# A transformer kernel on one core: unread products in TensorE's waits, and the first softmax maximum moved ahead of gates, key blocks and convolutions

## The chip, the core and the metric

The kernel runs on one core of a Trainium2 chip, as one program with one launch. TensorE (PE; its weight loads are shown as PEld), VectorE (DVE) and ScalarE (ACT) each run their own instruction list in order and wait for each other by semaphores; SyncE's queue (SP) issues the transfers, GpSimd (POOL) does nothing but four start-up instructions. The metric is the device time of one execution in microseconds (us). The kernel before takes 2849.9 us, the median of 3 runs (2849.38 to 2851.75).

## What is computed

Two blocks follow one another on a sequence of 256 tokens of width 1024, all in f32. The first has two layers of half-step feed-forward, token mixer, half-step feed-forward; the second adds 16 tokens (272 in all) and has an attention, a mixture of experts (MoE), a gated recurrence (`hgrn2`) and a second MoE. Cut to what the change touches:

```python
for l in range(DEPTH):                       # first block, DEPTH = 2
    h = modulate(rms_norm(x, norm_g[l, 0]), ...)
    x = x + 0.5 * gate * swiglu(h, ffn_w_in[l, 0], ffn_w_out[l, 0])
    h = modulate(rms_norm(x, norm_g[l, 1]), ...)
    x = x + gate * token_mix(h, ...)
    h = modulate(rms_norm(x, norm_g[l, 2]), ...)
    x = x + 0.5 * gate * swiglu(h, ffn_w_in[l, 1], ffn_w_out[l, 1])

def token_mix(h, ...):
    qkv, z, b_raw, a_raw, q_n, kc, vc, ks, vs, kw, vw, g_raw = split_cols(h @ w_in, IN_SIZES)
    y_gdn = gated_deltanet(qkv, z, b_raw, a_raw, ...)   # conv, silu, l2 norm; g from a_raw;
                                                        # chunks: (I + lower)^-1, then a scan
    y_nsa = native_sparse_attention(q_n, kc, vc, ...)   # three masked softmax branches:
                                                        # compressed keys, selected, window
    return concatenate([y_gdn, y_nsa]) @ w_out

# in native_sparse_attention
blk = t[:, cmp_idx] + pe[:, None, :]                    # key blocks of 32 tokens, stride 16
k_cmp = silu(blk @ w1) @ w2
# in gated_deltanet
g = -exp(a_log) * softplus(a_raw + dt_bias)             # the gates
```

The recurrence of the second block scans chunks with decayed scores, `o = o_inter + o_intra`, and carries a state.

## The kernel before

A `Block` gives every engine one long list. All engines walk over the same list of stages: `ada` (modulation), then per layer `ffn`, `mix`, `ffn`, then a norm, `fox` (attention), `moe`, `hg` (the recurrence), `moe`. Nothing reorders work afterwards: the order in which each engine's code is written is the order in which it runs. Weights come as slabs of 1 or 2 MB through a ring of 8 slots, issued by SP in one loop (L544) as slots come free.

**Waits.** `mark(ins, q, name, ...)` lets an instruction raise its engine's step semaphore, and `await_(engine, q, name, ...)` waits for that count. An engine stops at a wait with everything that stands behind it.

**Between stages.** The sums of squares of the norm are products with a matrix of ones (`ss_pair`, L1479 is its matmul); ScalarE makes the root from them (L2114, L2115), loads a table (L2156), VectorE scales (L3091), ScalarE shifts (L2121 or L2124), and, ahead of a feed-forward, VectorE makes the low part of a split f32 (L3184). Only then can TensorE begin: in a feed-forward with three products for each split pair (`up_split`, L1500 to L1502), in a mixer with projections (L825).

**In a mixer.** Projections and other products are "jobs" (`run_jobs`), four PSUM banks in turn, each read by ScalarE (L1684) or VectorE. After jobs 0 to 15 come 24 attention units. Unit n is `scores(n)` (PE L1036), `softmax_max(n)` (DVE: mask L2583, maximum L2587, negated L2597), `exp(n)` (ACT L1806), `turn(n)`, a transpose (PE L1053), a copy of it (ACT L1826), `values(n)` (PE L1068) and `output(n)` (DVE L2607 to L2624). `scores(n+1)` waits for the mask of unit n, since it overwrites the bank. Jobs are handed out between units by the table `MIX_STEPS`: 16, 17, 18, ... one for unit 0, one for unit 1 and so on. Jobs 16 and 17 are projections (8 products of 128x256 each); 18 and 19 are products of the key blocks (L775), for which VectorE writes `kp` in `block_keys` (four additions, L2337, behind a memset, L3237, and behind ScalarE's eight copies of `nsa_blocks`, L1790 and L1791). `gdn_gates` makes g (DVE L2318 to L2326, ACT L1657 to L1661), read from job 20 on. `conv(c)` is one of twelve column convolutions on VectorE (L2284, then L2287 three times); columns 0 and 1 are done ahead of `softmax_max(0)`, the others each after its projection.

**Behind the units** comes `gdn` with its levels: for each of 8 matrices products of 32x32 blocks, 32 products a group: L919 (p), L929 (up), L933 (tp), with ScalarE's copy L1733 between the first two. Level 0 waits for `lo` (DVE L2464). `gdn_values` (L888) and `turn_outputs` (L1088) lie between levels.

**In the recurrence** (`hg_scan`), for each of three token tiles t, levels from -1 up: score products (L1172 and others), one job (L816 or L825) behind each; at a tile's end it waits for `hsum` (ACT L1962) before the output products (L1202, L1205).

**Products for the clock** exist already: `keep_clock` (L1236) issues products that nobody reads, ahead of waits in the MoE's token sort.

An f32 product of `nc.tensor.matmul` shows as two MATMUL records and two LDWEIGHTS records in the trace; a product on split operands (`fp32r`, L1500 to L1502) as one of each.

## Time and profile before

| | |
|---|---|
| median of 3 runs | 2849.9 us |
| the profiled execution | 2847.29 us, of which its span 2845.5 us |
| PE busy | 2638.1 us (93%) |
| DVE busy / ACT busy | 1405.4 us (49%) / 775.1 us (27%) |
| mean granted TensorE clock | 0.969 |
| chain that ended last, by engine | PE 86%, DVE 6%, DMA 3%, ACT 3%, issue 1% |
| transfers | 701.51 MB, mean 247 GB/s |

The chain of work that ended last names, at each step back from the end, what released it. A time on it is on the path; idle time of other engines isn't. The line PEclk of the page shows the TensorE clock granted in 40 slices, in tenths of 2.4 GHz; in the table by stretches PEclk 1.00 is 2.4 GHz throughout and 0.50 is 1.2 GHz throughout, the only two levels that the records have.

### The profile page before, as it was taken

The page shows a single profiled execution, that of the slowest core. Times are in us where ns is not written, and L with a number is a line of the kernel's source. Part 1 is how long each engine was busy: PE and PEld are TensorE (multiplying, and loading weights), DVE is VectorE, ACT ScalarE, POOL GpSimd, SP SyncE. Part 2 cuts the span into 40 slices and gives each one's busy share as a digit, 9 for nine tenths or more (in the row PEclk, how much of TensorE's full clock was granted, in tenths as well). Part 3 has the DMA queues.
Part 4 walks back from the last instruction along what each step waited for, and adds up shares of the span by engine and source line. Part 5 has one row for each costly group of instructions (what it writes and reads, how often), then busy time and mean ns, then how long its engine had stood idle before and what let it go on. Part 6 is the DMA issues. An engine that isn't in the chain of part 4 may idle for free.

```text
span 2845.5 us, 44974 instructions
## 1 busy us (share of the span) xinstructions
PE 2638.1 (93%) x18582; PEld 1884.0 (66%) x18582; DVE 1405.4 (49%) x3071; ACT 775.1 (27%) x1473; POOL 0.2 (0%) x4
## 2 busy tenths in 40 slices
PE   6999988999999988999999999999999999999998
PEld 5998767998998767998777533333356784333333
DVE  7875764786773773663233333333324532333333
ACT  3332354334332352442233211111112321111110
POOL 0000000000000000000000000000000000000000
PEclk8999989999999989999999999999999999999999
DMA  8876211674766310454211599999961236999997
GB/s 351 302 277 267 105 46 60 265 297 193 296 268 237 119 60 33 186 222 168 75 67 38 198 377 427 428 427 427 428 243 60 90 119 269 418 428 427 427 428 307
DMA packets 72307, 701.51 MB, mean 247 GB/s; under 512 B 8736, under 2 KB 11424, under 8 KB 11680
## 3 DMA queue, kind: packets, MB, share of 16 engines
q1 hardware_dynamic: 72096, 698.54, 61.1%
q8 instruction: 152, 2.49, 0.3%
q14 instruction: 59, 0.48, 0.0%
HBM read 697.46 MB, written 1.05 MB: 245 GB/s over the span
## 4 chain that ended last, share of the span: by engine, by line
PE 86%; DVE 6%; DMA 3%; ACT 3%; issue 1%; DVEq 0%; SPq 0%; ACTq 0%
PE ps L1299 15%; PE ps L825 11%; PE ps L1500 9%; PE ps L1502 9%; PE ps L1501 9%; PE ps L1324 7%; PE ps L1340 5%; PE ps L816 4%; DMA ring<-slabs 3%; PE ps L1068 2%; PE ps L1269 1%; PE ps L1479 1%; PE ps L807 1%; PE ps L792 1%; PE ps L1053 1%
## 5 line engine op out<-in xcount | busy, mean ns | idle before, releaser
L1500 PE MATMUL ps<-arena_parts 128*128 128x256 f32 x2112 | 602.3, 285 | 35.0 <-DVE arena_parts L3184 35.0
L1502 PE MATMUL ps<-arena_parts,ring_parts 128*128 128x256 f32 x2112 | 598.8, 284 | 0.0
L1501 PE MATMUL ps<-arena_parts 128*128 128x256 f32 x2112 | 597.1, 283 | 0.0
L1299 PE MATMUL ps<-ring,arena 128*64 128x512 f32 x2048 | 467.1, 598 | 0.2 <-DMA ring<-slabs 0.2
L1500 PEld LDWEIGHTS ps<-arena_parts 128*128 128x128 f32 x2112 | 402.1, 190 | 36.6 <-DVE ring_parts L3099 20.7
L1501 PEld LDWEIGHTS ps<-arena_parts 128*128 128x128 f32 x2112 | 404.7, 192 | 0.2
L1502 PEld LDWEIGHTS ps<-arena_parts,ring_parts 128*128 128x128 f32 x2112 | 401.1, 190 | 0.0
L3099 DVE TENSOR_TENSOR ring_parts<-ring,arena_parts 128x2048 fp32r<-128x2048 f32 x132 | 300.9, 2291 | 112.8 <-ACT arena_parts L1647 112.8
L825 PE MATMUL ps<-h,ring 128*128 128x256 f32 (+1 forms) x1408 | 337.1, 398 | 9.4 <-ACT h L2124 5.9
L1647 ACT CAST arena_parts<-ring 128x2048 fp32r<-128x2048 f32 x132 | 250.0, 1904 | 301.1 <-DMA ring<-slabs 293.6
L2946 DVE TENSOR_TENSOR x<-ps,x 128x272 f32<-128x272 f32 x512 | 190.6, 434 | 263.3 <-PE ps L1340 250.7
L825 PEld LDWEIGHTS ps<-h,ring 128*128 128x128 f32 x1408 | 272.8, 197 | 58.2 <-issue 10.9
L1299 PEld LDWEIGHTS ps<-ring,arena 128*64 128x64 f32 x2048 | 136.5, 136 | 253.9 <-issue 253.0
L1324 PE MATMUL ps<-ring,arena 128*64 128x512 f32 x992 | 225.9, 596 | 25.9 <-ACT arena L2020 16.2
L1340 PE MATMUL ps<-arena 64*128 64x272 f32 x1024 | 167.5, 428 | 31.9 <-DVE x L2946 31.9
L2020 ACT ACTIVATE arena<-ps 128x256 f32<-128x256 f32 x64 | 24.6, 384 | 625.8 <-PE ps L1299 625.8
L1324 PEld LDWEIGHTS ps<-ring,arena 128*64 128x64 f32 x992 | 75.7, 136 | 169.8 <-issue 156.6
L732 DVE CUSTOM_DVE_ANT_0 ring<-ring,arena,vectors 128x1024 f32<-128x1024 f32 x144 | 177.0, 1280 | 10.2 <-DMA ring<-slabs 10.2
L1340 PEld LDWEIGHTS ps<-arena 64*128 64x128 f32 x1024 | 82.5, 185 | 140.7 <-DVE x L2946 84.5
L2924 DVE COPY arena<-ps 128x256 f32<-128x256 f32 x64 | 27.2, 425 | 203.5 <-PE ps L1308 203.5
L816 PE MATMUL ps<-ring,h 128*128 128x256 f32 (+3 forms) x576 | 120.0, 367 | 0.0
L816 PEld LDWEIGHTS ps<-ring,h 128*128 128x128 f32 (+1 forms) x576 | 86.6, 179 | 25.7 <-issue 6.8
(409 smaller groups left out, 2435.5 us busy)
## 6 DMA issues: line engine op xcount, KB each, us to landing
ring<-slabs SPq DMA_DIRECT2D x190, 2048.0 KB, 14.5
ring<-slabs SPq DMA_DIRECT2D x278, 1024.0 KB, 5.3
sq<-aside SPq DMA_DIRECT2D x2, 1024.0 KB, 7.9
arena<-aside SPq DMA_DIRECT2D x2, 1024.0 KB, 10.6
x<-xT SPq DMA_DIRECT2D x1, 1024.0 KB, 5.9
outT<-x SPq DMA_DIRECT2D x1, 1024.0 KB, 4.6
constants<-const SPq DMA_DIRECT2D x1, 875.0 KB, 7.8
vectors<-vec SPq DMA_DIRECT2D x1, 647.5 KB, 7.2
```

Source lines behind the costliest of these rows:

```text
L732: ins = nc.vector.tensor_tensor_reduce(out=wt[:, f], in0=wt[:, f], in1=cond_row, scale=1.0, scalar=col("ada_b", l * NADA + n), op0=ALU.mul ...
L816: mm = nc.tensor.matmul(ps[0:size, b, 0:width], rhs[:, k, at:at + size], wt[:, k, c0:c0 + width], start=(k == 0), stop=(k == KC - 1))
L825: mm = nc.tensor.matmul(bank(b, n), wt[:, k, c0:c0 + P], rhs[:, k, 0:n], start=(k == ks[0]), stop=(k == ks[-1]))
L1299: mm = nc.tensor.matmul(ps[W * hh:W * hh + W, e % 2, :], xe[:, e % 2, 4 * k + c], wt[:, c], start=(k == 0 and c == 0), stop=(k == 1 and c ...
L1324: mm = nc.tensor.matmul(ps[W * dh:W * dh + W, 3, :], hide[:, e % 2, j, W * hh:W * hh + W], wt[:, j, 512 * dh:512 * dh + 512], start=(hh == ...
L1340: mm = nc.tensor.matmul(ps[:, 4 + 2 * (i % 2) + dh, 0:T2], ysb[rows64, e % 2, i * P:(i + 1) * P], ge[rows64, e % 2], start=True, stop=True)
L1500: nc.tensor.matmul(out, w_hi, v_hi, start=start, stop=False, skip_group_check=True)
L1501: nc.tensor.matmul(out, w_hi, v_lo, start=False, stop=False, skip_group_check=True)
L1502: return nc.tensor.matmul(out, w_lo, v_hi, start=False, stop=stop, skip_group_check=True)
L1647: nc.scalar.copy(hi_slab(i), slab_view(i)).then_inc(s["w_hi"], 1)
L2946: nc.vector.tensor_tensor(x[:, d], ps[:, 4 + 2 * (i % 2) + dh, 0:T2], x[:, d], ALU.add)\
L3099: nc.vector.tensor_tensor(low_view(i), wt, hi_slab(i).bitcast(F32), ALU.subtract)\
```

## The change

Three things are changed. First, a new helper `unread(b, n)` issues n f32 products of 128x256 on constants into bank b, whose result nobody reads; it waits for nothing and raises nothing. It is called ahead of the first wait of each feed-forward (16 in the first, 8 in the other three), ahead of a mixer's first projections (5), ahead of `gdn` (4), inside `gdn` at level 1 (1 and 4), and in `hg_scan` (5 and 7 at tile 0, 5 at tiles 1 and 2, there behind a wait for `ho` that stood a few lines lower). That is 40 + 10 + 8 + 10 + 22 = 90 products. Second, in both mixers, VectorE does `softmax_max(0)` first, then the gates, and puts memset and key blocks behind `softmax_max(1)` and the convolutions of columns 0 and 1 behind units 1 and 2. Third, ScalarE does the copies of jobs 14 and 15 and `exp(0)` ahead of the gates and `nsa_blocks`. SP's list is the same.

```diff
@@ gdn (PE)
+                    if lev == 1:
+                        unread(6, 1)
                     await_("act", q, "p", lev)
                     await_("dve", q, "t", lev - 1)
...
                     mark(mm, q, "tp", lev)
+                    if lev == 1:
+                        unread(6, 4)
@@ hg_scan (PE)
                         b = 2 + (lev + 1) % 2
+                        if t == 0 and lev < 1:
+                            unread(6, 5 if lev < 0 else 7)
...
+                    if t:
+                        await_("act", q, "ho", t - 1)
+                        unread(6, 5)
                     await_("act", q, "hsum", t)
...
                     if t:
                         await_("dve", q, "hst", t - 1)
-                        await_("act", q, "ho", t - 1)
@@ new helper (PE)
+            def unread(b, n):
+                for _ in range(n):
+                    nc.tensor.matmul(bank(b, T1), ident, const[:, 0:T1], start=True, stop=True)
@@ the stages (PE)
                 if st[0] == "ffn":
+                    unread(2, 8 if t else 16)
...
                     pe.wait_ge(s["tables_in"], 32)
+                    unread(2, 5)
                     run_jobs(q, st, 0, 14, slab, job, h_at=("h_ready", n_ready - KC))
...
                     await_("dve", q, "o", n_units - 1)
+                    unread(6, 4)
                     gdn(q, st[1], st, slab, job)
@@ mixer (ACT)
                     exp, copy = attention(q, st)
-                    gdn_gates(q, st[1])
                     mix_task(q, st, 14)
                     mix_task(q, st, 15)
+                    exp(0)
+                    gdn_gates(q, st[1])
                     nsa_blocks(q, st[1], job)
-                    exp(0)
@@ mixer (DVE)
+                        softmax_max, output = attention(q, st)
+                        softmax_max(0)
                         gdn_gates(q, l)
-                        mark(nc.vector.memset(kp, 0.0), q, "kp0")
-                        await_("dve", q, "kp0")
-                        block_keys(q, l)
-                        softmax_max, output = attention(q, st)
-                        conv(q, l, 0)
-                        conv(q, l, 1)
                         await_("dve", q, "sg")
-                        softmax_max(0)
                         for n_unit in range(24):
                             if n_unit < 23:
                                 softmax_max(n_unit + 1)
                             if n_unit:
                                 output(n_unit - 1)
+                            if n_unit == 0:
+                                mark(nc.vector.memset(kp, 0.0), q, "kp0")
+                                await_("dve", q, "kp0")
+                                block_keys(q, l)
+                            if n_unit in (1, 2):
+                                conv(q, l, n_unit - 1)
```

VectorE's list in the first mixer before, from the last two instructions of the gates to the first softmax maximum (L3237 the memset, L2337 the key blocks, L2284 and L2287 the convolutions of columns 0 and 1, L2583 the mask, L2587 the maximum):

```order
L2322 SCALAR_TENSOR_TENSOR arena<-arena 128x8
L2326 SCALAR_TENSOR_TENSOR arena<-arena 128x8
L3237 MEMSET arena 128x1024
L2337 TENSOR_TENSOR arena<-arena,vectors 128x32x8
L2337 TENSOR_TENSOR arena<-arena,vectors 128x2x15x8
L2337 TENSOR_TENSOR arena<-arena,vectors 128x32x8
L2337 TENSOR_TENSOR arena<-arena,vectors 128x2x15x8
L2284 TENSOR_SCALAR arena<-arena,vectors 128x256
L2287 SCALAR_TENSOR_TENSOR arena<-arena,vectors 128x256 x3
L2284 TENSOR_SCALAR arena<-arena,vectors 128x256
L2287 SCALAR_TENSOR_TENSOR arena<-arena,vectors 128x256 x3
L2583 TENSOR_TENSOR arena<-ps,constants 128x2x128
```

The same place now, where VectorE's line numbers are 16 higher up to the mixer's body (L3251 is the reciprocal before the gates, L2599 the mask, L2603 the maximum, L2613 the negation, L2334 to L2342 the gates, L3262 the memset):

```order
L3251 RECIPROCAL arena<-arena 128x56
L2599 TENSOR_TENSOR arena<-ps,constants 128x2x128
L2603 TENSOR_REDUCE arena<-arena 128x2
L2613 TENSOR_SCALAR arena<-arena 128x2
L2334 TENSOR_TENSOR arena<-arena,vectors 128x8
L2336 SCALAR_TENSOR_TENSOR arena<-arena 128x8
L2338 SCALAR_TENSOR_TENSOR arena<-arena 128x8
L2342 SCALAR_TENSOR_TENSOR arena<-arena 128x8
L2599 TENSOR_TENSOR arena<-ps,constants 128x2x128
L2603 TENSOR_REDUCE arena<-arena 128x2
L2613 TENSOR_SCALAR arena<-arena 128x2
L3262 MEMSET arena 128x1024
```

The mask of unit 0 has moved from behind memset, key blocks and two convolutions to the front of the gates, and the mask of unit 1 stands ahead of the memset too. Behind the memset follow the key blocks, then the convolution of column 2 as before.

TensorE's list before, from the last values of the attention to level 2 of `gdn` (L1068 values, L919, L929 and L933 the groups of 32 small products, L888 the products of `gdn_values`):

```order
L1068 MATMUL ps<-arena 128x64 x4
L919 MATMUL ps<-constants,arena 32x32 x32
L888 MATMUL ps<-constants,arena 128x128 x8
L919 MATMUL ps<-arena 32x32 x32
L929 MATMUL ps<-arena 32x32 x32
L933 MATMUL ps<-arena 32x32 x32
L919 MATMUL ps<-arena 32x32 x32
```

The same place now (L1072 the values, L1249 the unread products, L931 and L935 what were L929 and L933):

```order
L1072 MATMUL ps<-arena 128x64 x4
L1249 MATMUL ps<-constants 128x256 x4
L919 MATMUL ps<-constants,arena 32x32 x32
L888 MATMUL ps<-constants,arena 128x128 x8
L919 MATMUL ps<-arena 32x32 x32
L1249 MATMUL ps<-constants 128x256
L931 MATMUL ps<-arena 32x32 x32
L935 MATMUL ps<-arena 32x32 x32
L1249 MATMUL ps<-constants 128x256 x4
L919 MATMUL ps<-arena 32x32 x32
```

Four products stand between the attention and level 0, one ahead of L931 and four ahead of level 2; nothing else has moved there.

## Rows read from the trace of the kernel before

**Rows 1.** The page, the granted clock in 40 slices.

```profile
PEclk8999989999999989999999999999999999999999
```

**Rows 2.** Waits of TensorE, whole span: line, waited for, us in total, times, longest.

```profile
PE ps L1500 <- DVE arena_parts L3184: 35.0, 4, 20.3
...
PE ps L1036 <- DVE arena L2583: 13.7, 4, 6.0
...
PE ps L825 <- ACT h L2124: 5.9, 2, 2.9
PE ps L1202 <- ACT arena L1962: 5.6, 2, 3.2
```

**Rows 3.** Stretches around the first units: length, busy by engine, PEclk, DMA share, GB/s.

```profile
289.50:295.50 6.00, 0.00 (x1) 0.01 (x1) 5.56 (x14) 0.09 (x1) 0.00 (x0) 0.90 0.01 1
295.50:302.94 7.44, 6.67 (x24) 5.17 (x24) 3.30 (x9) 2.34 (x11) 0.00 (x0) 0.62 0.00 0
...
942.12:946.91 4.79, 0.00 (x2) 0.00 (x1) 4.54 (x12) 0.00 (x0) 0.00 (x0) 0.93 0.03 10
946.91:954.54 7.63, 6.86 (x22) 5.30 (x22) 3.30 (x9) 2.34 (x11) 0.00 (x0) 0.60 0.00 0
```

**Rows 4.** Timeline of the first mixer: start, us, engine, line, operation, idle before.

```profile
285.78 3.72 PE L825 MATMUL ps<-h,ring 128*128 128x256 f32 x16
...
289.69 1.84 DVE L2337 TENSOR_TENSOR arena<-arena,vectors 128x256 f32<-128x256 f32 x4 [1.57 <-ACT arena L1791]
...
295.02 0.42 DVE L2583 TENSOR_TENSOR arena<-ps,constants 128x256 f32<-128x256 f32 x1
...
297.07 0.69 PE L1053 MATMUL ps<-constants,arena 128*128 128x128 f32 x2 [0.77 <-ACT arena L1806]
```

**Rows 5.** VectorE's timeline in the next units, first and last mask.

```profile
303.41 0.42 DVE L2583 TENSOR_TENSOR arena<-ps,constants 128x256 f32<-128x256 f32 x1 [4.16 <-PE ps L1036]
...
316.67 0.69 DVE L2583 TENSOR_TENSOR arena<-ps,constants 128x512 f32<-128x512 f32 x1 [0.87 <-PE ps L1036]
```

**Rows 6.** Stretches behind the waits at stage starts, columns as in rows 3.

```profile
234.86:241.00 6.14, 6.14 (x21) 5.12 (x22) 6.14 (x12) 3.03 (x8) 0.00 (x0) 0.72 0.00 0
...
489.31:493.50 4.19, 4.19 (x24) 4.19 (x25) 4.19 (x8) 4.19 (x5) 0.00 (x0) 0.65 0.00 0
...
690.03:695.00 4.97, 4.97 (x28) 4.97 (x29) 4.97 (x9) 4.97 (x5) 0.00 (x0) 0.64 0.00 0
...
1147.07:1152.00 4.93, 4.93 (x26) 4.93 (x27) 4.93 (x9) 4.93 (x5) 0.00 (x0) 0.60 0.00 0
```

**Rows 7.** TensorE's timeline, products of `keep_clock` at 2.4 GHz.

```profile
1586.90 2.46 PE L1236 MATMUL ps<-h,constants 128*128 128x272 f32 x10
```

**Rows 8.** Around the levels of `gdn`: stretches, then one row of TensorE's timeline.

```profile
406.04:408.25 2.21, 0.00 (x0) 0.03 (x1) 2.01 (x8) 2.19 (x2) 0.00 (x0) 0.50 0.01 4
408.25:425.54 17.29, 13.37 (x656) 11.85 (x657) 10.93 (x21) 3.31 (x10) 0.00 (x0) 0.54 0.02 5
...
1061.60:1079.31 17.71, 12.18 (x657) 10.52 (x657) 10.93 (x21) 3.31 (x10) 0.00 (x0) 0.79 0.01 4
...
416.83 0.44 PE L919 MATMUL ps<-arena 32*32 32x32 f32 x16 [1.53 <-issue]
```

**Rows 9.** The recurrence: two stretches, then rows of the timeline.

```profile
2170.68:2176.39 5.71, 5.71 (x39) 2.55 (x40) 1.62 (x9) 0.89 (x5) 0.00 (x0) 0.70 0.00 0
...
2231.63:2238.88 7.25, 7.25 (x55) 7.13 (x59) 0.00 (x0) 2.76 (x5) 0.00 (x0) 0.76 0.00 0
...
2161.24 7.20 DVE L2737 TENSOR_TENSOR_SCAN arena<-constants,arena 128x16 f32<-128x16 f32 x24
...
2170.68 0.56 PE L1172 MATMUL ps<-arena 128*16 128x16 f32 x16 [3.78 <-DVE arena L2789]
...
2287.78 1.36 DVE L2835 TENSOR_TENSOR h<-arena 128x1152 f32<-128x1152 f32 x1 [12.74 <-ACT arena L1974]
...
2289.63 2.62 PE L792 MATMUL ps<-h,ring 128*128 128x144 f32 x20
```

## The prediction, made before the changed kernel ran

> **What bounds the kernel now.** I read the page's shares first: TensorE is busy 93% and holds 86% of the chain that ended last, so what can be won is its idle time and the time in which it runs at the lower of its two clocks. The 40 slices of the clock [rows 1] show the second: 9 and 8 are spread over nearly the whole span, which reads as many short stretches at 1.2 GHz, one at a time, not as one slow stage.
>
> Next I read TensorE's waits [rows 2]. Four waits of the feed-forwards for L3184 hold 35.0 us, one of them 20.3, so the other three are 4.9 each. Two waits at the mixers' starts for ScalarE's L2124 are 2.9 each. The scores wait for VectorE's mask L2583 up to 6.0 us. Two waits in the recurrence for the row sums L1962 hold 5.6, the longer 3.2.
>
> Last I cut the span into stretches. In the wait of the second scores the clock is still 0.90 and 0.93, and in the 7.4 and 7.6 us behind it 0.62 and 0.60 [rows 3]: the clock falls after TensorE has idled, and the work behind pays. The same stands behind the waits at stage starts: 0.72, 0.65, 0.64, 0.60 [rows 6], and in the recurrence 0.70 and 0.76 [rows 9]. Work behind a wait loses (1 - clock) x length against full clock. Products with nothing to wait for, put into the wait, cost nothing as long as they end before the awaited result comes, and may keep the clock up.
>
> **What an unread product costs.** Ten records of `keep_clock`, five products of 272 columns, take 2.46 us at 2.4 GHz [rows 7], 0.49 each at most; 256 columns make it about 0.44, and at 1.2 GHz 0.87. Five take 2.2 us, seven 3.1, eight 3.5, sixteen 7.0.
>
> **A. VectorE's and ScalarE's order in the mixers.** Between the end of job 16 (289.50) and the start of scores(2) (302.94) lie 6.00 + 7.44 = 13.44 us [rows 3]. Only scores(1), turn(0) and job 17 stand in it. At full clock these are 6.67 x 0.62 = 4.1 us, or from above 3.72 for the job [rows 4], 0.69 / 2 = 0.35 for the turn and as much for the scores: 4.4. I take 4.4. The mask of unit 0 began at 295.02 behind key blocks (289.69) and two convolutions [rows 4]; by the new order it comes right behind the reciprocals, when scores(0) are done, before job 16 ends. `exp(0)`, which stood behind `nsa_blocks`, then also runs beside job 16, so the turn's 0.77 goes too. The gain is 13.4 - 4.4 = 9.0 here and 4.79 + 7.63 - 4.4 = 8.0 in the second mixer: 17.0. (The waits alone, 6.00 + 4.79 + 2 x 0.77, are 12.3; the other 4.7 is the clock.) The new unit 0 must wait for nothing else; about half a microsecond for the turn of unit 0 is my allowance: 16.5.
>
> What is moved back has to be done somewhere. The key blocks (1.84) and the two convolutions (from 289.69 + 1.84 to 295.02) end 5.3 us after they begin [rows 4]; the memset writes as many numbers as the key blocks and is bounded by their 1.84: up to 7.2 us. VectorE idles ahead of the masks of the next four units, first 4.16, last 0.87 us [rows 5], 8.9 in the four. So it fits, narrowly. The key blocks' reader is job 18, in unit 2: VectorE reaches them behind the mask of unit 1, some 6 us earlier in TensorE's work than job 18. The convolutions 0 and 1 and the gates are read only from job 20 on and later. If the cover were gone, masks would be late by what does not fit.
>
> **B. Mixer starts.** Five products, 2.2 us, in a wait of 2.9 [rows 2]: hidden, with 0.7 idle left. The 6.14 us behind ran at 0.72 [rows 6], a loss of 1.7; the second mixer's start is the same work behind the same wait, and I count it alike. Gain 2 x 1.7 = 3.4.
>
> **C. Feed-forward starts.** Eight products, 3.5 us, in waits of 4.9: hidden. Losses behind [rows 6]: 4.19 x 0.35 = 1.5, 4.97 x 0.36 = 1.8, 4.93 x 0.40 = 2.0; sum 5.2. But there TensorE reads what VectorE's L3184 still writes, one of eight parts after another, so a faster clock meets a wait for the next part; I take 4.0. The first feed-forward's sixteen products, 7.0 us in 20.3, leave 13 us idle behind them: 0.
>
> **D. Recurrence.** Tile 0, level -1: VectorE's scan L2737 (7.20 us for 24 [rows 9]) decides when level 0 starts; 0. Level 0: seven products, 3.1 us, in a wait of 3.78, and 5.71 us at 0.70 behind it: 1.7. Tile 1: five, 2.2 us, in a wait of 2.4 (5.6 - 3.2), and 7.25 us at 0.76 behind it: 1.7, less what spills over: 1.6. Tile 2: five in 3.2; L2835 ends at 2287.78 + 1.36 = 2289.14, and TensorE goes on at 2289.63 [rows 9], so faster products there win at most 0.5: 0.5. Sum 3.8.
>
> **E. `gdn`.** Here I expect a loss. Before level 0, TensorE waits 2.21 us with the clock at 0.50 already [rows 8]. The four products start when VectorE's last output is there, so at 0.87 each they take 3.5 us and outlast the wait by at least 1.3; that output ends inside the 2.21 us, which can make it some 0.6 more. I take 1.9 for each of two mixers: +3.8. The level chain behind it is as long at clock 0.54 (17.29 us) as at 0.79 (17.71) [rows 8]: 656 small records, the busy time 13.37 and 12.18, and the rest waits. So TensorE's rate does not set it; one wait reads "issue", 1.53 us [rows 8], that is, the next instructions weren't there. The five products of level 1 (2.2 to 4.3 us) lie beside that idle time, and a better clock gives nothing in the chain. From below, what follows the chain could run faster by what the clock is worth behind it; I estimate up to 1.4 for both. Net +2.4, with ends at +14 (2 x (1.9 + five products at 0.87 and one us for the wait behind them), nothing hidden) and -6 (8 less of the chain, as the third rival has it, beside the 2 that are lost ahead).
>
> The Trainium skill (page "Runtime: NRT & Kernel Launch", section "Instruction fetch mechanics") says that a long program is streamed in 16 KiB pieces and that crossing a boundary is "mostly hidden". The trace does not agree in this chain, with 1.53 us of "issue" in one place. By the page alone the chain would be TensorE's own, and a higher clock would shorten it; that is the third rival below.
>
> **Sum.** B, C and D are 3.4 + 4.0 + 3.8 = 11.2. The clock fell in places with far shorter idle too, so some of these stretches will be slow anyway: I take nine tenths, 10. In all 16.5 + 10 - 2.4 = 24.1. Against the profiled execution, 2847.3, that is 2823.2; the median of the runs is 2.6 higher, 2849.9, and the forecast against it 2825.8, so 2826.
>
> **Rivals.**
> First, the unread products don't hold the clock: they come right after an idle stretch or too few of them count. For it: the trace has no such products in a wait of this kind; those of `keep_clock` run at 2.4 GHz, but in another stage. Against: in the mixer the clock fell only where TensorE idled. Then heads (waits 12.3 and part of the clock, since shorter idle alone may not drop it: 16.5) and `gdn` with its loss: 2849.9 - 16.5 + 2.4 = 2835.8, say 2835.
>
> Second, VectorE's backlog. The moved 7.2 us don't fit into the gaps of 8.9, because with 9 us gone VectorE has lost that idle time too, and masks run late through the first units: up to 7.2 us come back in each mixer. 2826 + 14 = 2840. Against: between units stand more than four gaps.
>
> Third, the chain of `gdn` is TensorE's after all. At full clock its busy 13.37 x 0.54 is 7.2 us, with five products and the short waits some 13 us instead of 17.5: about 4 less for each, 8 for both, less what I took for it: 2819. Against: equal length at 0.54 and 0.79.
>
> Fourth, slower. The products run at 1.2 GHz because the clock has already fallen when they begin, don't raise it, and become the work that is waited for. Price 0.87 each, excess over the waits: feed-forwards 3 x (7.0 - 4.9) = 6, mixers 2 x (4.4 - 2.9) = 3, recurrence 6.1 - 3.8 and 2 x 4.4 - 5.6 and what lies beside L2737, 7 at most; `gdn` 2 x 5.7 = 11: 27. Against A's 16.5 this is +10, 2860. It decides once more than 17 of the 27 lie on the path. For it: the 0.50 in `gdn`. Against: elsewhere the clock was 0.90 and 0.93 in the wait itself [rows 3].
>
> That the change does not do what it says (the wait for the mask is replaced by one for ScalarE's copies of 14 and 15): 2845 to 2850.
>
> **How the numbers follow.** Forecast 0.57, first rival 0.18, second 0.07, third 0.12, fourth 0.03, last 0.03. The forecast's own range is 2820 to 2832, from `gdn`'s ends and B to D at half or whole. The range 2818 to 2838 takes in the first and third rival and leaves out somewhat under 0.2. What a measurement tells from no change is about 0.2%, 5.7 us: faster than 2844.2 has 0.92, the same 0.04, slower 0.04.
>
> **What would show it.** In the changed profile the first mask of each mixer follows the reciprocals at once, and TensorE's scores wait no 6.0 and 4.8 us for it; the stretch from the end of job 16 to scores(2) is 4 to 5 us. The stretches of [rows 6] and those of [rows 9] stand near 1.00, and the waits in [rows 2] read shorter by the products' time (4.9 to 1.4, 2.9 to 0.7). Level 0 of `gdn` begins 1 to 2 us after L2464's result, and its chain stays near 17 us. VectorE's gaps ahead of the masks of units 2 to 5 are nearly gone, but TensorE doesn't wait for them. Wrong would be: clocks of 0.6 to 0.7 behind the products (first rival), waits for masks of units 2 to 6 (second), a chain of 13 us (third), or L1249's records at half clock with the awaited result long there (fourth).

## The result and the profile after

| | before | changed |
|---|---|---|
| median | 2849.6 us | 2825.3 us (4 runs, 2820.5 to 2827.1) |
| ratio | | 0.991 (95%: 0.9893 to 0.9928) |
| profiled execution's span | 2845.5 us | 2823.3 us |
| PE busy | 2638.1 us | 2659.1 us |
| mean granted TensorE clock | 0.969 | 0.979 |

The kernel became 24.3 us faster; the forecast was 2825.8. Five later runs of the same changed kernel gave a median of 2827.1 (ratio 0.9912). TensorE is busy 21 us longer in a span that is 22.2 shorter: it now does 90 products more.

The page's clock slices [rows 1] after:

```profile
PEclk8999989999999999999999999999999999999999
```

Slice 15, which was 8, is 9 now, and nothing else shows: changes over stretches of a few microseconds hardly move a slice of 71. TensorE's waits after [rows 2], of the whole span (us in total, times, longest):

```profile
PE ps L1513 <- DVE arena_parts L3200: 18.3, 4, 14.0
...
PE ps L1040 <- DVE arena L2599: 2.9, 2, 1.4
...
PE ps L825 <- ACT h L2140: 1.5, 2, 0.8
...
PE ps L1210 <- ACT arena L1978: 1.3, 2, 1.1
PE ps L1249 <- DVE hid L2640: 1.2, 2, 0.6
```

The three shorter waits of the feed-forwards went from 4.9 to (18.3 - 14.0) / 3 = 1.4 us, those of the mixers from 2.9 to 0.8. The 6.0 and 4.8 us of the scores for the mask are gone; the 2.9 left on that line are two short waits that stood there before. One wait is new: the products ahead of `gdn` themselves wait 0.6 us for L2640. The stretches that answer to [rows 6], then to [rows 8], then to the two of [rows 9] (length, busy by engine, PEclk, DMA share, GB/s):

```profile
234.80:241.00 6.20, 6.13 (x29) 5.43 (x30) 6.20 (x12) 3.09 (x8) 0.00 (x0) 1.00 0.00 0
485.20:489.40 4.20, 3.64 (x29) 3.67 (x30) 4.20 (x10) 4.20 (x6) 0.00 (x0) 1.00 0.00 0
684.90:689.90 5.00, 4.51 (x36) 4.55 (x37) 5.00 (x9) 5.00 (x6) 0.00 (x0) 1.00 0.01 3
1130.70:1135.60 4.90, 4.79 (x38) 4.82 (x39) 4.90 (x9) 4.90 (x5) 0.00 (x0) 1.00 0.00 0
401.40:419.20 17.80, 12.62 (x667) 10.65 (x667) 9.04 (x17) 3.19 (x9) 0.00 (x0) 0.88 0.02 4
1046.64:1063.98 17.34, 12.41 (x667) 10.45 (x667) 9.04 (x17) 3.19 (x9) 0.00 (x0) 0.89 0.01 4
2150.00:2156.40 6.40, 5.95 (x49) 2.87 (x50) 2.04 (x11) 1.71 (x9) 0.00 (x0) 0.73 0.01 3
2211.30:2218.60 7.30, 7.10 (x117) 6.84 (x117) 1.41 (x6) 3.48 (x6) 0.00 (x0) 1.00 0.01 2
```

Behind every stage's start the clock is 1.00 where it was 0.60 to 0.72, and so it is in the recurrence's tile 1. In tile 0 it is 0.73 where it was 0.70: there the prediction failed, as term D below tells. The level chain of `gdn` has 0.88 and 0.89 for 0.54 and 0.79 and is as long as before.

TensorE in the first mixer, against [rows 4] (start, us, then what the row is):

```profile
285.42 3.72 PE L825 MATMUL ps<-h,ring 128*128 128x256 f32 x16
289.07 0.49 PE L1040 MATMUL ps<-arena 64*128 64x128 f32 x4
289.49 0.44 PE L1057 MATMUL ps<-constants,arena 128*128 128x128 f32 x2
289.76 3.62 PE L825 MATMUL ps<-h,ring 128*128 128x256 f32 x16
293.31 0.49 PE L1040 MATMUL ps<-arena 64*128 64x128 f32 x4
```

No row has an idle time before it, which would stand at its end in brackets. From the end of job 16 (289.1) to scores(2) (293.31) it is 4.2 us, where it was 13.4. VectorE beside it, against [rows 4] and [rows 5]:

```profile
285.53 0.43 DVE L2599 TENSOR_TENSOR arena<-ps,constants 128x256 f32<-128x256 f32 x1 [1.26 <-PE ps L1040]
...
289.67 0.42 DVE L2599 TENSOR_TENSOR arena<-ps,constants 128x256 f32<-128x256 f32 x1 [1.31 <-PE ps L1040]
...
291.86 1.90 DVE L2353 TENSOR_TENSOR arena<-arena,vectors 128x256 f32<-128x256 f32 x4
...
295.40 0.42 DVE L2599 TENSOR_TENSOR arena<-ps,constants 128x256 f32<-128x256 f32 x1
...
304.80 0.68 DVE L2599 TENSOR_TENSOR arena<-ps,constants 128x512 f32<-128x512 f32 x1
```

The masks wait for scores only in units 0 and 1; from 290.9 to 309.8 VectorE works without a gap. The 8.9 us of [rows 5] are used up, and TensorE does not wait for it.

**Where the time went, stretch by stretch.** Each figure is the difference in time between the same two of TensorE's instructions, against the first profile of before. "Again" are second profiles of the same code; the last column is the changed kernel without any product in `gdn`.

| stretch | before again | changed | changed again | order only | products only | no `gdn` products |
|---|---|---|---|---|---|---|
| first mixer's start (50 us) | 0.0 | -0.4 | -1.7 | +1.2 | -1.7 | -0.4 |
| first head (17.5 us) | -0.4 | -9.2 | -9.2 | -9.2 | +1.0 | -9.2 |
| attention behind it, up to its last values | 0.0 | +0.6 | +2.3 | +0.6 | 0.0 | +0.6 |
| ahead of first `gdn` | 0.0 | +2.1 | +2.1 | 0.0 | +2.1 | 0.0 |
| first `gdn`'s chain | +1.1 | +0.5 | +1.6 | +0.4 | +0.6 | +2.3 |
| behind it, to feed-forward | +1.8 | +2.8 | +1.1 | +1.2 | +1.1 | +3.5 |
| three feed-forward starts | -0.1 | -4.1 | -4.1 | -0.3 | -4.1 | -4.1 |
| second mixer's start | 0.0 | -1.7 | -1.7 | 0.0 | -1.7 | -1.7 |
| second head | 0.0 | -8.3 | -8.2 | -8.2 | +0.7 | -8.2 |
| attention, ahead of second `gdn` | 0.0 | +1.0 | +1.1 | -1.1 | +1.8 | -1.1 |
| second `gdn`'s chain | +1.7 | -0.4 | +1.3 | +0.7 | -0.4 | +0.4 |
| behind it | -1.4 | -0.9 | -2.7 | -1.0 | -3.3 | +0.4 |
| `fox` | -0.2 | -3.1 | +0.4 | +3.0 | -1.6 | -3.0 |
| recurrence's three tiles | +1.2 | -1.8 | -1.8 | +1.2 | -1.7 | -3.5 |

The heads with the new order, the feed-forward starts with all their products and the step ahead of the first `gdn` repeat to 0.1 us in every kernel that has the same code there. Most other rows move by 1 to 3.5 us without any change of code.

### The profile page after: what moved, and what is told of

Read it like the earlier page. It is cut to its first block, busy times and chain, and to the rows that moved or that the text cites. A ratio compares the mean times of both kernels' runs of the same rounds, so it can differ in the third digit from the quotient of the medians.

```text
span 2823.3 us, 45331 instructions
## 1 busy us (share of the span) xinstructions
PE 2659.1 (94%) x18762; PEld 1901.8 (67%) x18762; DVE 1404.0 (50%) x3071; ACT 774.9 (27%) x1473; POOL 0.2 (0%) x4
## 4 chain that ended last, share of the span: by engine, by line
PE 85%; DVE 6%; DMA 4%; ACT 3%; issue 1%; DVEq 0%; SPq 0%; ACTq 0%
PE ps L1312 14%; PE ps L825 11%; PE ps L1513 9%; PE ps L1515 9%; PE ps L1514 9%; PE ps L1337 7%; PE ps L1353 5%; DMA ring<-slabs 4%; PE ps L816 4%; PE ps L1072 2%; PE ps L1492 1%; PE ps L1282 1%; PE ps L807 1%; PE ps L792 1%; PE ps L1057 1%
## 5 line engine op out<-in xcount | busy, mean ns | idle before, releaser
L1513 PE MATMUL ps<-arena_parts 128*128 128x256 f32 x2112 | 600.3, 284 | 18.3 <-DVE arena_parts L3200 18.3
L825 PE MATMUL ps<-h,ring 128*128 128x256 f32 (+1 forms) x1408 | 327.0, 390 | 5.0 <-DVE h L3107 3.5
L825 PEld LDWEIGHTS ps<-h,ring 128*128 128x128 f32 x1408 | 265.4, 191 | 50.8 <-issue 6.6
L816 PEld LDWEIGHTS ps<-ring,h 128*128 128x128 f32 (+1 forms) x576 | 85.6, 177 | 24.3 <-issue 4.6
```

Source lines behind the costliest of these rows:

```text
L816: mm = nc.tensor.matmul(ps[0:size, b, 0:width], rhs[:, k, at:at + size], wt[:, k, c0:c0 + width], start=(k == 0), stop=(k == KC - 1))
L825: mm = nc.tensor.matmul(bank(b, n), wt[:, k, c0:c0 + P], rhs[:, k, 0:n], start=(k == ks[0]), stop=(k == ks[-1]))
L1513: nc.tensor.matmul(out, w_hi, v_hi, start=start, stop=False, skip_group_check=True)
```

## The experiments

The diffs are against the changed kernel; `...` stands for lines left out.

**The order alone.** All `unread` calls taken out, the order of the change kept.

```diff
-                    unread(2, 8 if t else 16)
...
-                    unread(2, 5)
...
-                    unread(6, 4)
```

> The new order of VectorE and ScalarE in the mixers, no unread products. Theory (terms add): the order alone gives the 16.5 to 17.8 us that its stretches show, so 2832 to 2833 us against 2849.6. Rival (VectorE's backlog comes back as waits later in the mixer): 2840 or more. Rival (products and order depend on each other, since the clock in the mixers falls again without products): gain under 14 us, 2836 or more.

Measured: 2835.4 us, ratio 0.9946 (0.9932 to 0.9961), 15.4 us won against 2850.8 for before in the same comparison: somewhat less than the 16.5 to 17.8 expected, and more than the rival's 14. Its heads gave 9.2 and 8.2, so the order alone carries the whole of term A. Its waits at the starts stayed:

```profile
PE ps L1506 <- DVE arena_parts L3190: 34.3, 4, 19.7
...
PE ps L825 <- ACT h L2130: 5.8, 2, 2.9
```

No backlog followed. Of 17.4 in the heads 15.4 arrived in the median; the differences that do not repeat (+3.0 in `fox`, for one) cover that.

**The products alone.** The old order of VectorE's and ScalarE's mixer, all 90 products.

```diff
                     exp, copy = attention(q, st)
+                    gdn_gates(q, st[1])
                     mix_task(q, st, 14)
                     mix_task(q, st, 15)
+                    nsa_blocks(q, st[1], job)
                     exp(0)
-                    gdn_gates(q, st[1])
-                    nsa_blocks(q, st[1], job)
...
+                        gdn_gates(q, l)
+                        mark(nc.vector.memset(kp, 0.0), q, "kp0")
+                        await_("dve", q, "kp0")
+                        block_keys(q, l)
                         softmax_max, output = attention(q, st)
+                        conv(q, l, 0)
+                        conv(q, l, 1)
+                        await_("dve", q, "sg")
                         softmax_max(0)
-                        gdn_gates(q, l)
-                        await_("dve", q, "sg")
...
-                            if n_unit == 0:
-                                mark(nc.vector.memset(kp, 0.0), q, "kp0")
-                                await_("dve", q, "kp0")
-                                block_keys(q, l)
-                            if n_unit in (1, 2):
-                                conv(q, l, n_unit - 1)
```

> All 90 unread products, the old order of VectorE and ScalarE. The prediction's terms: 10 won at the stage starts and in the recurrence, 2.4 lost in gdn: 2842. By the changed kernel's trace (gdn cost about 7 us, not 2.4, in the two mixers together): 4 to 5 us won, 2845. Rival (the products hold no clock): 2849.6 + 2.4 or more, 2852.

Measured: 2843.7 us, ratio 0.9976 (0.9963 to 0.9989), 7.1 us won, between the two values expected (2842 and 2845). The products do hold a clock. The parts add: 15.4 + 7.1 = 22.5, against 24.3 for both. The scores' wait is what it was:

```profile
293.95 0.80 PE L1040 MATMUL ps<-arena 64*128 64x128 f32 x4 [5.99 <-DVE arena L2599]
```

Its second `gdn` shows the chain at almost full clock:

```profile
1063.16:1080.50 17.34, 11.93 (x668) 9.98 (x667) 9.27 (x18) 3.19 (x9) 0.00 (x0) 0.98 0.02 4
```

17.34 us at 0.98, with five products more in it, against 17.29 at 0.54 [rows 8].

**Without the products of `gdn`, and without the four ahead of it alone.** In the second kernel only the last of these three calls is taken out.

```diff
-                    if lev == 1:
-                        unread(6, 1)
...
-                    if lev == 1:
-                        unread(6, 4)
...
-                    unread(6, 4)
                     gdn(q, st[1], st, slab, job)
```

> The changed kernel without the nine products of each gdn (four ahead, one and four at level 1); nothing else differs from it. Prediction's term E: 2.4 us faster than the changed kernel, 2823. Changed kernel's trace: 5 to 7 us faster, 2818 to 2820. Rival (the products of gdn pay by a higher clock behind): 2 to 6 us slower, 2827 to 2831.

> The changed kernel without the four products ahead of gdn alone; the one and four at level 1 stay. If the level chain is bound by the supply of its instructions, the five at level 1 cost nothing and the head is the whole loss: as fast as the kernel without any gdn products, within 1 us, 2819 to 2820. If the chain pays for them too: only 4 us of the gain, about 1.5 to 3 us slower than without any.

Measured: 2822.7 us (0.9902, 0.9887 to 0.9918) without any, 2825.7 (0.9916, 0.9903 to 0.993) without the four. Without any product in `gdn` the kernel is 2.6 and 4.4 us faster than the changed kernel's two medians; term E says 2.4. Without the four alone it is no faster than the changed kernel, and 3.0 slower than without any, with runs that nearly separate (2818.6 to 2823.5 without any, 2823.2 to 2828.9 without the four). By the expectation that is a chain that pays for its five products. The traces, of executions only 0.5 us apart (2822.7 and 2823.2), say something else. The first row is the changed kernel's, the second that without the four:

```profile
397.69 3.78 PE L1249 MATMUL ps<-constants 128*128 128x256 f32 x8 [0.62 <-DVE hid L2640]
```

```profile
400.08 1.08 PE L919 MATMUL ps<-constants,arena 32*32 32x32 f32 x64 [2.22 <-DVE arena L2479]
```

The products wait 0.6 and run 3.8 us, at 1.2 GHz, in place of a wait of 2.2: 2.1 us lost in each mixer. The chain without any product is not shorter in the traces: over the seven kernels and repeats without products in `gdn` (14 chains, the changed kernel's variants below included) it is 17.3 to 19.6 us, mean 18.5; over the five with nine products (10 chains) 17.3 to 19.0, mean 18.2. With the five of level 1 alone, without the four ahead, the two chains are 18.9 and 19.4. So five products at level 1 cost nothing by the traces and 3 us by the medians, and which holds is open.

Nor do they simply fill the "issue" waits, of which this is one without any product:

```profile
406.60 0.91 PE L919 MATMUL ps<-arena 32*32 32x32 f32 x58 [1.36 <-issue]
```

Added up over a chain these waits are 2.5 to 5.2 us without products (mean 3.8) and 3.0 to 4.9 with nine (mean 4.2). What has become shorter is the chain's other work: TensorE was busy 13.37 us of the first chain before, at 0.54, and is 12.62 us now, at 0.88, with the five products in it. Without products no chain ran above 0.79, so what the clock alone would give isn't shown.

What does keep the chain's length can be read from the queue that brings instructions. Before, in the 22 us from 404 on, in slices of 0.55 us:

```profile
GB/s 0 0 0 0 0 0 15 0 0 0 30 0 0 0 0 0 0 0 30 0 0 0 0 0 0 30 0 0 0 0 0 30 0 0 0 0 0 0 0 30
...
q8 instruction: 5, 0.08, 1.5%
```

Each 30 is one piece of instructions, 0.016 MB; the view does not name their engine. They come 3.6 to 4.4 us apart here, and 3.3 to 4.7 us apart in all 26 chains that have no more than five products inside, at clocks from 0.50 to 0.98. That fits a chain whose length is set by the arrival of its instructions; no run changed their number.

**Fifteen products at level 1.**

```diff
                     if lev == 1:
-                        unread(6, 4)
+                        unread(6, 14)
```

> The changed kernel with fourteen unread products instead of four ahead of level 2 of gdn (ten more in each of two mixers). Theory (the level chain is bound by the supply of TensorE's instructions: its idle time marked issue, 4.2 us, goes where the products are): the chain from the first L919 to L807 grows from 17.8 and 17.3 by at most 2 us, the waits marked issue behind the products vanish, the kernel 2 to 4 us slower. Rival (TensorE-bound): it grows by ten times 0.44, 4.4 us each, the waits marked issue stay, the kernel 9 us slower.

Measured: 2830.8 us, ratio 0.9942 (0.9923 to 0.9962). The kernel is 3.7 to 5.5 us slower than the changed one, between theory and rival. The chains are 21.3 and 21.7 us, 3.5 and 4.3 longer than in the changed kernel's first profile and 3.1 and 3.5 longer than the mean of 18.2, for 4.4 us of work. The rows (first `gdn`):

```profile
407.57 6.31 PE L1249 MATMUL ps<-constants 128*128 128x256 f32 x28
...
422.04 0.56 PE L935 MATMUL ps<-arena 32*32 32x32 f32 x41 [1.72 <-issue]
```

Here my theory failed: the issue waits behind the products did not vanish (0.68 and 1.72 us follow). Ten more products are paid for by three quarters or so. The queue of the instructions shows what they do, 404 to 426 again:

```profile
GB/s 0 30 0 0 0 0 0 0 30 0 0 0 0 0 0 0 0 0 0 0 0 30 0 0 0 0 0 0 30 0 0 0 0 0 0 30 0 0 0 0
```

As long as the 28 records ran no piece came, for 7.5 us (7.0 in the second mixer), and behind them the pieces come 3.7 and 3.8 us apart as before. That ties them to TensorE's list. So the supply of instructions did not use that time to get ahead, and the idle times behind the products stayed.

**`exp(0)` back behind the gates.**

```diff
-                    exp(0)
                     gdn_gates(q, st[1])
                     nsa_blocks(q, st[1], job)
+                    exp(0)
```

> The changed kernel with ScalarE's exp(0) back behind gates and nsa_blocks; VectorE keeps the new order. Theory (VectorE's mask was the wait, ScalarE's place is worth the short rest): the head of each mixer, 8.3 us after the change, grows by 0.5 to 1.5 us, the kernel 1 to 3 us slower. Rival (ScalarE's place matters as much, since nsa_blocks and the gates then hold exp(0) up and the clock falls again): 4 us or more for each head.

Measured: 2826.5 us (0.9924, 0.9908 to 0.9941), within the noise of the changed kernel's 2825.3 and 2827.1. The heads are 1.25 and 1.23 us longer, as the theory said, by one wait each:

```profile
289.62 0.44 PE L1057 MATMUL ps<-constants,arena 128*128 128x128 f32 x2 [1.18 <-ACT arena L1822]
```

So VectorE's order is worth 15.0 of the heads' 17.4, the place of `exp(0)` 2.5 once VectorE's is there.

**Half the products.**

```diff
-                            unread(6, 5 if lev < 0 else 7)
+                            unread(6, 2 if lev < 0 else 3)
...
-                        unread(6, 5)
+                        unread(6, 2)
...
-                    unread(2, 8 if t else 16)
+                    unread(2, 4 if t else 16)
...
-                    unread(2, 5)
+                    unread(2, 2)
```

> The changed kernel with about half the products at each place but gdn and the first feed-forward (4 for 8, 2 for 5, 2 and 3 for 5 and 7). Theory (the time TensorE is idle just before the awaited work decides): the low clock comes back behind most waits, the starts' segments go back to what they are without products: 1.1 to 1.7 us each, 7 to 9 us in all slower. Rival (any product in the wait does): no difference. A third reading: the shorter waits (2.9) still hold with half and the longer (4.9) do not.

Measured: 2831.2 us (0.9942, 0.9925 to 0.9959), some 4 to 6 slower than the changed kernel, with runs from 2826.2 to 2844.0; the profile is of one at 2841.9. It is neither all nor nothing. The second and the fourth feed-forward lost the clock (+1.4 and +1.0 against before, where the full number gives -1.1 and -1.6), and both mixers' starts too (0.0 and 0.0). The third feed-forward (-1.4) and the recurrence's tile 1 (-1.6) kept all. (Two later profiles with all five products, the first of the kernel with products in more waits and that of the kernel with products at the mixers' ends alone, also show 0.0 for the second mixer's start, but there the clock is 1.00 behind the start and falls 39 us later.) The fourth feed-forward, its first product and then the stretch behind:

```profile
1139.96 0.55 PE L1513 MATMUL ps<-arena_parts 128*128 128x256 f32 x1 [3.16 <-DVE arena_parts L3200]
```

```profile
1139.96:1145.00 5.04, 5.04 (x23) 5.04 (x24) 5.04 (x9) 5.04 (x5) 0.00 (x0) 0.50 0.02 3
```

3.16 us of idle time are left in front and the clock falls. In front of the third feed-forward the same 3.16 us are left, and the clock stays:

```profile
690.18 0.36 PE L1513 MATMUL ps<-arena_parts 128*128 128x256 f32 x1 [3.16 <-DVE arena_parts L3200]
```

```profile
690.18:695.20 5.02, 5.02 (x40) 5.02 (x41) 5.02 (x9) 5.02 (x5) 0.00 (x0) 1.00 0.01 3
```

So the idle time just before the work doesn't decide alone; what else does wasn't found.

**Products in more waits.** No `gdn` products (their removal is left out of the diff); five ahead of the first sum-of-squares pair behind each mixer, six ahead of the attention's norm, three ahead of the first projections of the attention and the recurrence.

```diff
+                if pair == 0 and stages[q - 1][0] == "mix":
+                    unread(6, 5)
                 pe.wait_ge(s["sq_ready"], 4 * nb + pair + 1)
...
+                if st[0] == "fox":
+                    unread(6, 6)
                 for pair in range(summed[q], 4):
                     ss_pair(q, pair)
+                if st[0] in ("fox", "hg"):
+                    unread(6, 3)
```

> The changed kernel without gdn's products, and with products in other waits: five ahead of the first sum-of-squares pair behind each mixer's output (wait 2.45 us), six ahead of the attention's norm (2.98), three ahead of the first projections of the attention and of the recurrence (1.8 each). Theory: each wait's stretch at the low clock behind it (1.7 us for 3.4 at 1.2 GHz) goes at the two mixers' ends and in front of the attention, 5 us, at best 8: 2815 to 2818. Rival (the clock falls a little later anyway, as it did after the first mixer's start): within 2 us of the kernel without gdn products, 2821 to 2824.

Measured: 2820.3 us (0.9895, 0.9879 to 0.9912), with one run at 2828.8 and three at 2817.8 to 2820.3; the profile is of the one. The median lies between theory (2815 to 2818) and rival (2821 to 2824). So it was run again beside the changed kernel:

> The kernel with products in more waits a second time, beside the changed kernel on the same chip, since its first profile fell on an execution 8 us above its other three. Theory: 2818 to 2821, 4 to 6 us below the changed kernel. Rival: its median is within 2 us of the changed kernel's, what it wins at the mixers' ends is lost again ahead of the attention.

> The changed kernel a second time, to see which differences between its stretches and those of before repeat. Theory: heads (-9.2, -8.3), feed-forward starts (-1.1, -1.4, -1.6), the second mixer's start (-1.7) and the wait ahead of gdn (+2.1) come back to 0.1 us; the first mixer's start, the stretch behind gdn, the attention and its surroundings differ by 1.5 to 3 us from execution to execution, since the clock falls there at other places. Rival: every stretch repeats, then the 2.8 us behind gdn and the 3.1 in the attention belong to the change. Median 2823 to 2827.

Measured: 2820.6 us (2819.4 to 2821.4) against 2827.1 (2822.5 to 2829.7) for the changed kernel on the same chip; the runs don't overlap. So this version is 6.5 us faster than the changed kernel; that it is faster than the one without any `gdn` products (2822.7, on another chip) isn't shown. A wait of 2.45 us behind the first mixer is 2.32 of products and 0.29 of waiting:

```profile
466.15 2.32 PE L1245 MATMUL ps<-constants 128*128 128x256 f32 x10
468.76 1.13 PE L1490 MATMUL ps<-sq,constants 128*128 128x256 f32 x4 [0.29 <-ACT sq L2128]
```

The changed kernel's second profile sorts the differences as its theory said, `fox` above all: 3.1 us won in one profile and 0.4 lost in the other. The stretch's clock is the difference (changed, then changed again):

```profile
1327.84:1539.03 211.19, 204.94 (x1090) 153.96 (x1089) 72.84 (x263) 69.80 (x258) 0.00 (x0) 0.96 0.17 60
```

```profile
1327.87:1542.63 214.76, 208.51 (x1091) 156.69 (x1090) 72.37 (x262) 69.32 (x258) 0.00 (x0) 0.94 0.17 59
```

**Products at the mixers' ends alone.** As the version above, without those around the attention and the recurrence.

```diff
-                if st[0] == "fox":
-                    unread(6, 6)
...
-                if st[0] in ("fox", "hg"):
-                    unread(6, 3)
```

> The changed kernel without gdn's products and with five products ahead of the first sum-of-squares pair behind each mixer alone. Theory: the head of gdn gives 4.2, the mixer ends 1.4 and 2.3 as their stretches showed, the lost cover in gdn's chain takes some 1.5 back: 2819 to 2821. Rival (the products around the attention are what made the version with more waits fast): 2822 to 2825, like the one without gdn products.

Measured: 2828.6 us (0.9927, 0.9912 to 0.9941), 8 above the version with all of them and outside both expectations. `fox` took 4.2 us longer than before in its profile, where the other took 1.6 less. It is also 5.9 slower than the kernel without any `gdn` products, from which it differs by the products at the mixers' ends alone. These give 1.3 and 2.3 us in their own stretches, and `fox`, whose code is the same in both, takes 7.7 us more. So a stretch that nobody touched outweighs what was won. Whether the twelve products around the attention and the recurrence prevent that, or which of them, wasn't tried.

**Before again.**

> The kernel before a second time, for its stretches. Theory: heads, starts and the wait ahead of gdn repeat to 0.1 us; stretches with many short idle times (attention tails, behind gdn, fox) move by 1.5 to 3 us without any change of code. Rival: all repeat to 0.3 us.

Measured: 2850.5 us (ratio 1.0, 0.999 to 1.001). Starts and second head repeat to 0.15 us, the first head to 0.4; chains and what is behind them move by 1.1 to 1.8. The recurrence's tile 2 took 1.3 us longer. So neither expectation held whole: the theory named the right kind of stretch for `gdn`, but the attention in the mixers (0.0) and `fox` (-0.2) repeated here.

## Why the prediction was right, term by term

**A, the order (16.5; measured 17.4).** Right in place and mechanism, and the allowance of 0.5 us wasn't needed: 9.2 and 8.2 where 9.0 and 8.0 stood before it. The order alone and the two profiles of the changed kernel show it to 0.1. The moved work fitted into VectorE's gaps, so the second rival is out.

**B, mixer starts (3.4; measured 2.1 in one profile, 3.4 in the other).** Behind the first wait the clock was held both times. What differs came 38 us later. In the changed kernel's first profile TensorE ran fifteen us without any idle time before it, and the clock still fell at 273.2:

```profile
258.00:273.20 15.20, 15.20 (x118) 14.63 (x118) 8.49 (x17) 2.03 (x3) 0.00 (x0) 1.00 0.92 357
273.20:276.60 3.40, 3.40 (x10) 2.77 (x10) 3.13 (x6) 0.25 (x1) 0.00 (x0) 0.50 0.94 359
```

The products L1019 that stand there took 4.94 us; in the second profile 3.27. Of the ten profiles with all five products five show this fall between 272 and 274 us, and -0.4 for the first mixer's start; the other five show -1.7.

**C, feed-forward starts (4.0; measured 4.1).** 1.1, 1.4 and 1.6, the same in every kernel with full products, 0.3 at most without them.

**D, recurrence (3.8; measured 1.8 against the first profile of before, 3.0 against the second).** Tile 0's level 0 was taken at 1.7 and gave nothing (+0.1). The step that failed is the one that counted the wait as fixed. The products kept the clock for the job before them, TensorE came 1.5 us earlier to its wait for VectorE's scan and what follows it, and these end when they end: from the products of level -1 to those of level 0 it is 9.29 us before and after. So the wait grew: 3.29 us of products and still 2.04 of idle time, and the clock fell behind it.

```profile
2145.12 3.29 PE L1249 MATMUL ps<-constants 128*128 128x256 f32 x14
2150.45 0.60 PE L1178 MATMUL ps<-arena 128*16 128x16 f32 x16 [2.04 <-DVE arena L2805]
2150.89 5.11 PE L816 MATMUL ps<-ring,h 128*16 128x256 f32 x16
```

Tile 1 gave 1.6 as forecast (3.3 in five of the variants, whose code is the same there), tile 2 0.3 for 0.5 against the first profile of before. In the second, and in the kernel with the order alone, tile 2 is 1.3 us longer, so the gain there is 0.3 or 1.6.

**E, `gdn` (2.4 lost; measured 4.2 lost ahead of it by the traces, 2.6 and 4.4 in all by the medians).** The head was forecast at 1.9 for each mixer and is 2.1. The chain is not shorter with products than without beyond its spread, and without them it is as long at 0.79 as at 0.54; at 0.98, with its five products, it took 17.34 us, not the rival's 13. So the third rival, and with it what the Trainium skill's page "Runtime: NRT & Kernel Launch" (section "Instruction fetch mechanics") would make of it, did not come: a wait marked issue of 1.3 to 2.2 us stood in every chain. (That rival's end of the range, -6, sets only 2 against the 8 won; with the 3.8 of this term it is -4.2.) The 1.4 us of gain behind the chain that I set against the head wasn't seen: there the two profiles of the changed kernel differ by 1.7 us in either mixer, and those of before by 1.8 and 1.4. Whether the five products of level 1 are free stays open, as said above.

**The sum.** By the repeating terms it is 17.4 + 2.1 + 4.1 + 1.8 - 4.2 = 21.2 for the first profile, where 22.2 were measured between the profiles; by the forecast 24.1, and 24.3 in the medians. So the closeness of the total is in part luck: B to D came out at 8.0 for the 10 forecast and E cost 1.8 more. Against these 3.8 us stand 0.9 in A, 1.0 in stretches that nobody touched, and 2.1 from the profiled executions' places among the runs: that of before lay 2.4 below its median, that of the changed kernel 0.2.

The first rival (products don't hold the clock) falls with C; the fourth (products at 1.2 GHz as the work waited for) is real in one place, `gdn`, where it was priced as the forecast's own.

## What to carry to other kernels

Look first for the engine whose list puts work with a far reader ahead of work with a near one: here moving it cost next to nothing and gave two thirds of the gain. Products in a wait paid here where the clock was still high when they began, where they left 1.4 us or less of it idle, and where they ended before the result came; with 2.0 us left the clock fell, with 3.2 in two places of three, and where they began at 1.2 GHz and outlasted the wait they cost 2.1 us; count the waits anew after each gain, since work that now runs faster makes the next wait longer. Profile the same kernel twice before a difference of 1 to 3 us in one stretch is explained; `fox` alone, in two kernels with the same code there, differed by 7.7.

## What the runs showed of the hardware that was not expected

- The granted clock fell to 1.2 GHz after 15.2 us in which TensorE's records left no idle time, and in a second execution of the same code it did not.
- Half as many products held the clock behind the third feed-forward's start and lost it behind the second's and the fourth's, with the same 3.16 us of idle time before the third as before the fourth.
- A chain of 656 records, 640 of them of 32x32 products, took 17.3 to 19.6 us at clocks from 0.50 to 0.79, and 17.3 to 19.4 at 0.77 to 0.98 with five unread products inside.
- In these chains pieces of 0.016 MB of instructions came 3.3 to 4.7 us apart at any clock, and none came for 7.0 and 7.5 us while 28 records of unread products ran.
